# A paged-attention score loop: every second group of pages in partitions 32 to 127

## The chip, the core and the metric

The kernel runs on one core of a Trainium2 chip. TensorE (PE) multiplies into PSUM, VectorE (DVE) and ScalarE (ACT) move and compute, GpSimd (POOL) and SyncE (SP) issue transfers here. Sixteen DMA engines move the data between HBM and SBUF, whichever engine issues a transfer. The metric is the device time of one execution in microseconds (us), as the median of several runs. The profile comes from one further execution.

## The reference, cut to what matters

One inference step of a two-layer decoder: 512 prompt tokens and 8 sample tokens go through half feed-forward layers, a mixer and again a half feed-forward layer. The first layer's mixer has latent attention (MLA) beside a gated recurrence (HGRN2). For the 8 sample tokens the attention reads a paged cache of 4096 past positions each, 32 pages of 128 rows, found through a page table:

```python
q_lat = jnp.einsum('bshn,chn->bshc', q_nope, w_uk)
ckv_past = pool_ckv[layer_idx, page_table].reshape(db, -1, A_KV_LORA)     # 256 wide
kpe_past = pool_kpe[layer_idx, page_table].reshape(db, -1, A_ROPE)        # 32 wide
sc_past = (jnp.einsum('bshc,btc->bhst', q_lat, ckv_past)
           + jnp.einsum('bshr,btr->bhst', q_pe, kpe_past)).astype(jnp.float32) * SM_SCALE
...
p = jax.nn.softmax(jnp.concatenate([sc_past, sc_self], axis=-1), axis=-1).astype(ckv.dtype)
o_lat = (jnp.einsum('bhst,btc->bshc', p[..., :n_past], ckv_past)
         + jnp.einsum('bhst,btc->bshc', p[..., n_past:], ckv))
```

The score is a dot product over 256 + 32 = 288 rows. All data is float32.

## The kernel before

The time falls into three parts. Before about 550 us stand the first feed-forward layer, the input projection and the queries; after about 885 us the output projection, three feed-forward layers and the second mixer. Both are long rows of 128x128x260 matmuls on PE (L278 to L280), with weights that SP loads through three buffers (`stream`, L495). Between them, in some 330 us, the HGRN2 recurrence, the keys and values of the prompt and the prompt's attention run, and the whole cache is read beside them. The change touches only this middle part.

**Pages.** The host stores each page twice: transposed for the scores (three slices of 96 rows, `SR` = 96, `SK` = 3, so 96 partitions of 3 x 128 numbers) and as it is for the values (128 partitions of 256 numbers). A job is two pages (`JOB` = 2), a group is four jobs (`COLG` = 4), a sequence has four groups (`QUADS`), and there are 32 groups, here numbered 0 to 31. The score buffers `s_raw` and the value buffers `v_raw` are rings of eight jobs (`RING`), so of two groups: even groups lie in buffers 0 to 3, odd ones in 4 to 7.

**Who loads.** `load_job` (L457) issues one transfer per page, in `@block.sync` (SP) for all score pages and for every fourth job of value pages, in `@block.gpsimd` (POOL) for the other three. SP's order is fixed by the loop at `for k in range(COLG, S_JOBS + LAG)`: eight score transfers of a group n, then two value transfers of group n - 5 (`LAG` is 20 jobs), then group n + 1. Each score group starts with a wait on `s_done`, so with the scores of group n - 2, each pair of value transfers with a wait on `v_done`. Page numbers are read from SBUF into registers (`page_numbers`, L481).

**Who computes.** PE works through one list of instructions. `sample_to(k)` is called between the steps of the recurrence (`hgrn`), of the keys (`keys`) and of the prompt (`prompts`), and puts the scores of a group (L1685, 24 matmul records: three slices by four jobs, each job into its own 32 columns of the array), the values of a group (L1700) and steps of the softmax between them. During the recurrence that is one group in each of the 16 steps. The recurrence itself goes from PE (L1784) through eight dependent DVE operations (L1285) and back.

**Sample queries.** `sample_queries` on DVE clears `q_s` and fills it: the rotary rows (L1157), then three copies from PSUM (L1162). `q_s_ready` counts these to `Q_S_STEPS`; PE waits for it ahead of the first scores, POOL ahead of `state_in(0)`. These DVE operations stand just ahead of the recurrence's first DVE chain.

## Time and profile before

| | us |
|---|---|
| median of 3 runs (2272.53 to 2280.35) | 2275.16 |
| profiled execution, its own time | 2284.63 |
| its span, first to last instruction | 2282.9 |
| PE busy in the span | 2185.3 (96%) |
| DVE, ACT, POOL busy | 1036.6, 730.8, 120.2 |
| score pages loaded, 256 transfers of 144 KB | 37.7 MB |
| value pages loaded, 256 transfers of 128 KB | 33.6 MB |

The profiled execution is 9.5 us (0.4%) above the median and lies 1.7 us above its own span. In 40 slices of 57 us, PE is 90% busy or more except in slices 11 to 15 (571 to 856 us), the middle part, where the DMA engines' share goes up to its highest. An engine's busy time leaves out the issuing of transfers, so SP has no busy time at all in these views; what SP does is seen in the timeline and in the waits of the DMA queue's own engine.

### The profile page before, as it was taken

To read this page: it belongs to the slowest core of one execution; us is meant where nothing else is said; L and a number is where in the kernel's file an instruction comes from. 1 tells how busy PE (TensorE), PEld (TensorE's weight loads), DVE (VectorE), ACT (ScalarE), POOL (GpSimd) and SP (SyncE) were. 2 spreads that over 40 slices of the span, in tenths; PEclk is the share of its full clock that TensorE was granted. 3 is DMA by queue.
4 is the path that set the end of the run, shared out by engine and by line. 5 is a ranking of instruction groups with operands and counts; after the bars stand their busy time and mean duration, and the time that the engine had idled before them with its cause. 6 is when DMAs were issued, how large, how long until landed. Compare 5 with 4: busy or idle time off the path is not lost.

```text
span 2282.9 us, 46816 instructions
## 1 busy us (share of the span) xinstructions
PE 2185.3 (96%) x18285; PEld 2072.4 (91%) x18285; DVE 1036.6 (45%) x2002; ACT 730.8 (32%) x1292; POOL 120.2 (5%) x226
## 2 busy tenths in 40 slices
PE   8999999998776789999999999999999999999997
PEld 8999999997443458999999999999999999999997
DVE  5444434366654344544433444443446664444333
ACT  6222223354212333422222232222232233222222
POOL 0000000001234241000000000000000000000000
PEclk9999999998887789999999999999999999999999
DMA  4222223234799872222222222222322222222222
GB/s 162 92 92 92 92 102 100 81 125 147 213 265 279 236 212 93 84 92 92 92 92 100 97 91 91 92 92 92 102 92 92 92 93 92 88 87 91 94 100 75
DMA packets 101037, 261.98 MB, mean 115 GB/s; under 512 B 14385, under 2 KB 49218, under 8 KB 100866
## 3 DMA queue, kind: packets, MB, share of 16 engines
q1 hardware_dynamic: 89746, 228.83, 31.6%
q0 software_dynamic: 11184, 31.69, 4.7%
q8 instruction: 72, 1.18, 0.2%
q14 instruction: 35, 0.29, 0.0%
HBM read 255.29 MB, written 5.16 MB: 114 GB/s over the span
## 4 chain that ended last, share of the span: by engine, by line
PE 61%; DVE 1%; ACT 0%; issue 0%; DVEq 0%; ACTq 0%
PE bank L279 20%; PE bank L278 20%; PE bank L280 20%; PE bank L1929 1%; PE bank L1908 0%; PE bank L303 0%; DVE sb_x L1012 0%; PE bank L1921 0%; PE bank L1700 0%; PE bank L1943 0%; DVE sb_x L373 0%; ACT L312 0%; ACT sb_t L343 0%; DVE sb_h_lo L351 0%; ACT sb_h_hi L338 0%
## 5 line engine op out<-in xcount | busy, mean ns | idle before, releaser
L278 PE MATMUL bank<-sb_h_hi,sb_w_hi 128*128 128x260 f32 x3552 | 1005.9, 283 | 9.8 <-DVE sb_h_lo L1471 8.2
L279 PE MATMUL bank<-sb_h_lo,sb_w_hi 128*128 128x260 f32 x3552 | 1007.1, 284 | 0.0
L280 PE MATMUL bank<-sb_h_hi,sb_w_lo 128*128 128x260 f32 x3552 | 1003.8, 283 | 0.0
L250 ACT ACTIVATE sb_w_hi<-sb_raw 128x1024 fp32r<-128x1024 f32 x339 | 359.7, 1061 | 1260.8 <-PE bank L280 1257.1
L278 PEld LDWEIGHTS bank<-sb_h_hi,sb_w_hi 128*128 128x128 f32 x3552 | 668.5, 188 | 11.5 <-DVE sb_w_lo L256 8.3
L280 PEld LDWEIGHTS bank<-sb_h_hi,sb_w_lo 128*128 128x128 f32 x3552 | 671.4, 189 | 0.0
L279 PEld LDWEIGHTS bank<-sb_h_lo,sb_w_hi 128*128 128x128 f32 x3552 | 668.1, 188 | 0.2
L256 DVE TENSOR_TENSOR sb_w_lo<-sb_raw,sb_w_hi 128x1024 fp32r<-128x1024 f32 x339 | 415.3, 1225 | 382.4 <-ACT sb_w_hi L250 381.6
L279 PE MATMUL bank<-sb_a_lo,sb_w_hi 128*128 128x260 f32 x1408 | 399.1, 283 | 0.0
L278 PE MATMUL bank<-sb_a_hi,sb_w_hi 128*128 128x260 f32 x1408 | 398.7, 283 | 0.0
L280 PE MATMUL bank<-sb_a_hi,sb_w_lo 128*128 128x260 f32 x1408 | 397.7, 282 | 0.0
L280 PEld LDWEIGHTS bank<-sb_a_hi,sb_w_lo 128*128 128x128 f32 x1408 | 265.1, 188 | 0.0
L278 PEld LDWEIGHTS bank<-sb_a_hi,sb_w_hi 128*128 128x128 f32 x1408 | 264.9, 188 | 0.0
L279 PEld LDWEIGHTS bank<-sb_a_lo,sb_w_hi 128*128 128x128 f32 x1408 | 264.5, 188 | 0.0
L980 DVE TENSOR_TENSOR sb_t<-bank,sb_t 128x260 f32<-128x260 f32 x176 | 75.3, 429 | 261.1 <-PE bank L280 258.3
L972 DVE TENSOR_TENSOR sb_t<-bank,sb_r 128x260 f32<-128x260 f32 x176 | 74.4, 425 | 221.3 <-PE bank L280 200.7
L466 POOL DMA_DIRECT2D sb_v_raw<-in_cache x192 | 103.8, 541 | 195.0 <-PE bank L1700 176.2
L1685 PE MATMUL bank<-sb_s_raw,sb_q_s 96*32 96x256 f32 x768 | 60.1, 449 | 16.0 <-DMA sb_s_raw<-in_cache 8.8
L278 PE MATMUL bank<-sb_m_hi,sb_w_hi 128*128 128x260 f32 x256 | 73.2, 286 | 0.8 <-DVE sb_m_lo L1454 0.8
L279 PE MATMUL bank<-sb_m_lo,sb_w_hi 128*128 128x260 f32 x256 | 73.2, 286 | 0.0
L280 PE MATMUL bank<-sb_m_hi,sb_w_lo 128*128 128x260 f32 x256 | 73.0, 285 | 0.0
L985 DVE TENSOR_TENSOR sb_a_lo<-sb_t,sb_a_hi 128x260 f32 (+1 forms) x176 | 67.1, 423 | 0.0
(279 smaller groups left out, 1556.3 us busy)
## 6 DMA issues: line engine op xcount, KB each, us to landing
sb_raw<-in_w SPq DMA_DIRECT2D x339, 512.0 KB, 3.5
sb_s_raw<-in_cache SPq DMA_DIRECT2D x256, 144.0 KB, 4.7
sb_v_raw<-in_cache POOLq DMA_DIRECT2D x192, 128.0 KB, 5.3
sb_v_raw<-in_cache SPq DMA_DIRECT2D x64, 128.0 KB, 5.8
sb_x<-in_x SPq DMA_DIRECT2D x4, 520.0 KB, 6.2
out_y<-sb_x SPq DMA_DIRECT2D x8, 260.0 KB, 2.3
sb_st<-in_state POOLq DMA_DIRECT2D x8, 256.0 KB, 8.2
out_state_s<-sb_st POOLq DMA_DIRECT2D x8, 256.0 KB, 5.7
```

What stands on the lines that cost most here:

```text
L250: nc.scalar.activation(w_hi[slot][:], raw[slot][:], ACT.Copy).then_inc(S("w_hi_done"), 1)
L256: nc.vector.tensor_tensor(w_lo[slot][:], raw[slot][:], w_hi[slot][:], ALU.subtract).then_inc(S("w_lo_done"), 1)
L278: nc.tensor.matmul(out, wh, xh, start=first and c == 0, stop=False)
L279: nc.tensor.matmul(out, wh, xl, start=False, stop=False)
L280: mm = nc.tensor.matmul(out, wl, xh, start=False, stop=last and c == chunks - 1)
L466: eng.dma_start(slots[k % RING][0:rows, j, :], dram["cache"][bass.ds(page_numbers[j], 1), lo:lo + rows * width].rearrange("a (p w) -> (a p ...
L972: dve.tensor_tensor(t1[:, half[hf]], pair(g, hf), r[:, half[hf]], ALU.mult) \
L980: dve.tensor_tensor(t3[:, half[hf]], pair(g + 1, hf), t2[:, half[hf]], ALU.mult) \
L985: dve.tensor_tensor(a_lo[:, ff, half[hf]], t3[:, half[hf]], a_hi[:, ff, half[hf]], ALU.subtract) \
L1685: last = mm(out, q_s[0:SR, i, c, :], s_raw[(COLG * n + j) % RING][0:SR, :, c * P:(c + 1) * P], start=q % 2 == 0 and c == 0, stop=q % 2 == ...
L1929: last = mm(bank[3][:, b * P:(b + 1) * P], v_t[:, k, vals], prob_t[:, tri(b) + k, :], start=k == 0, stop=k == b)
```

## The change

Even groups stay as they are. A page of an odd group is loaded in two pieces: its rows 32 to 95 (64 rows) to partitions 32 to 95, and its rows 0 to 31 (32 rows) to partitions 96 to 127. Partitions 0 to 31 of buffers 4 to 7 are cleared once by POOL, and the scores of odd groups multiply over all 128 partitions. For this `q_s` gets a copy of its rows 0 to 31 in rows 96 to 127, by a fourth DVE copy. `Q_S_STEPS` goes up by one, and PE waits once for the clearing (`s_cleared`), ahead of group 1.

```diff
-        Q_S_STEPS = SK + 2
+        Q_S_STEPS = SK + 3
+        LOW = P - SR
...
             rows, lo, width = (SR, 0, S_W) if kind == "s" else (PAGE, SR * S_W, KV_LORA)
+            pieces = ((0, 0, rows),) if kind == "v" or k // COLG % 2 == 0 else ((LOW, LOW, SR - LOW), (SR, 0, LOW))
             for j in range(JOB):
-                eng.dma_start(slots[k % RING][0:rows, j, :],
-                              dram["cache"][bass.ds(page_numbers[j], 1), lo:lo + rows * width].rearrange("a (p w) -> (a p) w", w=width)) \
-                    .then_inc(loaded(kind, k), 16)
+                for to, row, count in pieces:
+                    first = lo + row * width
+                    eng.dma_start(slots[k % RING][to:to + count, j, :],
+                                  dram["cache"][bass.ds(page_numbers[j], 1), first:first + count * width].rearrange("a (p w) -> (a p) w", w=width)) \
+                        .then_inc(loaded(kind, k), 16)
...
-                eng.wait_ge(loaded("s", COLG * q), 16 * JOB * COLG * uses)
+                eng.wait_ge(loaded("s", COLG * q), 16 * JOB * COLG * uses * (1 + q % 2))
...
             state_in(1)
+            pool.wait_ge(S("half_done"), 2 * U0["ukv"])
+            for i in range(COLG, RING):
+                pool.memset(s_raw[i][0:LOW], 0.0).then_inc(S("s_cleared"), 1)
             pool.wait_ge(S("q_lat_mm"), 1)
...
+                dve.wait_ge(S("q_s_ready"), Q_S_STEPS - 1)
+                dve.tensor_copy(q_s[SR:P, :, :, 0:HEADS], q_s[0:LOW, :, :, 0:HEADS]).then_inc(S("q_s_ready"), 1)
...
+                rows = slice(0, SR if n % 2 == 0 else P)
+                if n == 1:
+                    pe.wait_ge(S("s_cleared"), COLG)
...
-                        last = mm(out, q_s[0:SR, i, c, :], s_raw[(COLG * n + j) % RING][0:SR, :, c * P:(c + 1) * P],
+                        last = mm(out, q_s[rows, i, c, :], s_raw[(COLG * n + j) % RING][rows, :, c * P:(c + 1) * P],
```

On SP, the start of group 1 (the first odd group) read as follows before. DMA rows name the buffer and the shape that is written; ISA rows are register work.

```order
L481 TENSOR_LOAD sb_pages_67 [waits half_done]
L466 ISA
L466 DMA sb_s_raw4_155<-in_cache 96x384
L466 ISA
L466 DMA sb_s_raw4_155<-in_cache 96x384
L466 ISA
L466 DMA sb_s_raw5_156<-in_cache 96x384
```

Now the same place reads:

```order
L485 TENSOR_LOAD sb_pages_67 [waits half_done]
L470 ISA
L470 DMA sb_s_raw4_155<-in_cache 64x384
L470 REGISTER_ALU
L470 DMA sb_s_raw4_155<-in_cache 32x384
L470 ISA
L470 DMA sb_s_raw4_155<-in_cache 64x384
L470 REGISTER_ALU
L470 DMA sb_s_raw4_155<-in_cache 32x384
L470 ISA
L470 DMA sb_s_raw5_156<-in_cache 64x384
```

Each page of an odd group is now two transfers, with a register operation ahead of each: 16 transfers a group where there were 8, and all 16 odd groups are like this one. The even groups are unchanged.

On DVE, the end of the sample queries and the start of the recurrence's chain (`sb_s_ring`) read before:

```order
L1157 COPY sb_q_s<-sb_q_t 32x8x8 [waits att_cleared]
L1162 COPY sb_q_s<-bank 96x8x8 [waits q_lat_mm]
L1162 COPY sb_q_s<-bank 96x8x8
L1162 COPY sb_q_s<-bank 64x8x8
L1282 COPY sb_s_ring<-bank 128x128 [waits state_mm]
L1285 SCALAR_TENSOR_TENSOR sb_s_ring<-sb_s_ring,sb_decay,bank 128x128 [waits state_step] x7
```

and now:

```order
L1169 COPY sb_q_s<-bank 96x8x8 [waits q_lat_mm]
L1169 COPY sb_q_s<-bank 96x8x8
L1169 COPY sb_q_s<-bank 64x8x8
L1172 COPY sb_q_s<-sb_q_s 32x24x8 [waits q_s_ready]
L1291 COPY sb_s_ring<-bank 128x128 [waits state_mm]
```

One copy with a wait for the copies before it stands between the sample queries and the recurrence. On POOL, between the loads of two sample states and the value pages of group 1, there are four new rows:

```order
L556 DMA sb_st1_120<-in_state 128x512
L580 MEMSET sb_s_raw4_155 32x768 [waits half_done]
L580 MEMSET sb_s_raw5_156 32x768
L580 MEMSET sb_s_raw6_157 32x768
L580 MEMSET sb_s_raw7_158 32x768
L485 TENSOR_LOAD sb_pages_67 [waits q_lat_mm]
```

The value pages of group 1 stand behind four clears on POOL; nothing else on POOL has moved.

## Rows read from the trace of the kernel before

**Rows 1.** Windows, whole core: length, busy us (count) per engine, PEclk, DMA share, GB/s

```profile
core 0: us, PE busy (x) PEld busy (x) DVE busy (x) ACT busy (x) POOL busy (x), PEclk, DMA share, GB/s
580.00:590.00 10.00, 7.73 (x94) 3.79 (x94) 5.71 (x17) 3.46 (x10) 0.00 (x0) 1.00 0.78 233
620.00:684.00 64.00, 49.62 (x544) 27.35 (x544) 33.06 (x105) 13.32 (x44) 24.17 (x45) 0.90 1.08 264
812.00:840.00 28.00, 22.81 (x224) 15.87 (x225) 11.47 (x37) 8.60 (x23) 12.12 (x22) 0.94 1.03 263
862.00:869.00 7.00, 5.75 (x54) 4.69 (x53) 4.01 (x15) 3.67 (x12) 3.20 (x6) 1.00 0.90 330
```

**Rows 2.** Waits of PE, 560 to 880 us: us in total, times, longest

```profile
PE bank L1784 <- DVE sb_s_ring L1285: 19.2, 10, 4.5
PE bank L1685 <- DMA sb_s_raw<-in_cache: 8.8, 5, 3.9
...
PE bank L1700 <- DMA sb_v_raw<-in_cache: 1.7, 2, 1.2
```

**Rows 3.** Timeline of SP, 616 to 690 us: start, length, transfers in a row

```profile
616.82 3.86 SPq L466 DMA_DIRECT2D sb_s_raw<-in_cache  x8
621.38 0.90 SPq L466 DMA_DIRECT2D sb_v_raw<-in_cache  x2
623.26 5.34 SPq L466 DMA_DIRECT2D sb_s_raw<-in_cache  x8
...
683.86 4.65 SPq L466 DMA_DIRECT2D sb_s_raw<-in_cache  x8
```

**Rows 4.** Waits of SP: 566 to 620, 620 to 684, 690 to 810, 809 to 830 us

```profile
SPq L466 <- PE bank L1685: 18.8, 6, 7.6
...
SPq L466 <- PE bank L1685: 12.8, 8, 2.8
...
SPq L466 <- PE bank L1685: 47.6, 10, 9.6
...
SPq L466 <- PE bank L1685: 5.4, 1, 5.4
```

**Rows 5.** Transfers of score pages, 620 to 684 us: issue ns, and time to landing

```profile
L466 SPq DMA_DIRECT2D sb_s_raw<-in_cache x59: 317/317/1424, 619.9 to 683.9; - x59
...
DMA to landing us min/median/max: 5.0/8.0/11.2
```

**Rows 6.** Timeline of DVE, POOL and PE, 556 to 603 us

```profile
556.55 0.52 DVE L1162 COPY sb_q_s<-bank 96x64 f32<-96x64 f32 x3
...
559.53 3.52 POOL L466 DMA_DIRECT2D sb_v_raw<-in_cache  x6 [0.82 <-issue]
602.48 1.13 POOL L466 DMA_DIRECT2D sb_v_raw<-in_cache  x2 [39.43 <-PE bank L1700]
...
560.05 2.08 PE L1784 MATMUL bank<-sb_v_blk,sb_kdv 64*128 64x512 f32 x4 [4.50 <-DVE sb_s_ring L1285]
570.25 1.48 PE L1685 MATMUL bank<-sb_s_raw,sb_q_s 96*32 96x256 f32 x24
```

**Rows 7.** POOL's memset of 128x1024; score and value matmuls, ns min/median/max

```profile
L581 POOL MEMSET sb_q_bd<- x1: 971/971/971, 690.2 to 690.2; 128x1024 f32 x1
...
L1685 PE MATMUL bank<-sb_s_raw,sb_q_s x768: 376/379/636, 563.7 to 840.4; 96*32 96x256 f32 x192
...
L1700 PE MATMUL bank<-sb_v_raw,sb_p_t x512: 376/379/634, 600.6 to 871.2; 128*32 128x256 f32 x171
```

**Rows 8.** Timeline of SP and PE, 809 to 832 us: groups 29, 30 and 31

```profile
809.40 3.95 SPq L466 DMA_DIRECT2D sb_s_raw<-in_cache  x8
814.04 0.90 SPq L466 DMA_DIRECT2D sb_v_raw<-in_cache  x2
815.68 4.28 SPq L466 DMA_DIRECT2D sb_s_raw<-in_cache  x8
820.66 1.03 SPq L466 DMA_DIRECT2D sb_v_raw<-in_cache  x2
822.43 5.12 SPq L466 DMA_DIRECT2D sb_s_raw<-in_cache  x8
828.24 0.90 SPq L466 DMA_DIRECT2D sb_v_raw<-in_cache  x2
...
829.91 1.56 PE L1685 MATMUL bank<-sb_s_raw,sb_q_s 96*32 96x256 f32 x24 [3.91 <-DMA sb_s_raw<-in_cache]
```

## The prediction

> **What bounds the kernel now.** Outside 550 to 885 us PE is 90% busy or more, and the change touches nothing there. Inside, I read the windows first: the DMA engines are saturated from 620 to 684 us (share 1.08, 264 GB/s) and again from 812 to 840 us (1.03, 263 GB/s) [rows 1]. The page transfers are what fills them: a group is 8 x 144 KB of scores and 8 x 128 KB of values, 2.23 MB, and at 264 GB/s that takes 8.4 us. Then the waits of PE: in 320 us it stands 8.8 us for score pages and 1.7 us for value pages, together 10.5 us, and 19.2 us for the recurrence on DVE [rows 2]. So the DMA engines are full for a stretch, but PE idles little for them directly. All that a perfect transfer could give back is about those 10.5 us, 0.5% of the kernel.
>
> The third view is SP, which no busy time shows. From 616.82 to 683.86 us it starts eight groups, one in 67.0 / 8 = 8.4 us [rows 3]. In each it spends 3.86 us on eight score transfers (0.50 us from one issue to the next, of which the transfer instruction is 0.317 us [rows 5] and the rest register work), 0.90 us on two value transfers, and 0.7 us on page numbers ahead of each. Some blocks are longer (5.34 instead of 3.86 us), since a single issue can take up to 1.42 us. Its free time is what it waits for the scores of two groups back: 12.8 us between 620 and 684 us [rows 4]. So SP works (67.0 - 12.8) / 8 = 6.8 us of each 8.4 us. It is the second engine here with hardly any room.
>
> **What the change does to SP.** This is the term that decides. Odd groups get 8 more issues. A 96-row transfer costs 0.50 us from issue to issue. Smaller pieces are not in the trace; fewer rows might take a little less, long issues come in proportion. The bounds are 0.42 us (the instruction's 0.317 us and half of the register work) and 0.55 us (0.50 us and a share of long issues); I take 0.48 us, nearer to the row that there is, with 0.25 us of long issues in a group: 8 x 0.48 + 0.25 = 4.1 us more per odd group, 2.05 us per group. Four stretches:
> - 566 to 616.82 us, groups 2 to 8 on SP: three odd ones add 12.3 us. SP's waits there are 18.8 - 7.6 = 11.2 us (the longest, 7.6 us, lies before group 2) [rows 4]. It starts the saturated stretch 12.3 - 11.2 = 1.1 us late at least, and not all free time is where it is needed: I take 1.5 us (1 to 4).
> - 616.82 to 684 us: 6.8 + 2.05 = 8.85 us of work per group against the 8.4 us between groups: 0.5 us x 8 groups = 4 us (at 0.42 us an issue 6.8 + 1.7 = 8.5, so 1 us; at 0.55 us with the long issues 6.8 + 2.4 = 9.2, so 6.5 us). PE's next scores wait for these pages, the pages two groups on wait for the scores, and so the delay stays.
> - 690 to 810 us: SP waits 47.6 us [rows 4]; six odd groups at most add 25 us. Covered by the keys' and prompt's work on PE: 0 (0 to 1).
> - 809 to 829 us: SP's only wait (5.4 us) lies ahead of group 29 [rows 4, 8]. Then it works through to 829.14 us, and odd groups 29 and 31 add 4.1 us each. The pages of group 30 would be issued by 824.1 instead of 820.0 us; PE took them at 829.91 us, after a wait of 3.91 us [rows 8]. 5.8 us is more than the smallest time to landing but less than the median of 8.0 us [rows 5]. I take 1.3 us (0 to 3).
>
> **The other parts.** The copy of `q_s` on DVE stands ahead of the chain for which PE waits 4.50 us at 560.05 us [rows 6], so it counts in full. Three copies of 64 numbers take 0.52 us [rows 6]; one of 192 with a wait for its predecessors is 0.2 to 0.6 us: 0.4 us. The four clears on POOL: 768 numbers each, against 971 ns for 1024 [rows 7], so 0.73 x 4 = 2.9 us. They delay the value pages of group 1 from 559.53 us, behind which POOL idles 39.43 us [rows 6]: nothing. They end by 563 us, and PE's scores of group 1, which now wait for them, start at 570.25 us [rows 6]: nothing. Matmuls over 128 instead of 96 partitions: 379 ns in both rows [rows 7], nothing. What an extra transfer costs the DMA engines themselves has no row: 16 transfers share a group's 8.4 us, 0.53 us each, and since the bytes stay the same, the 8 extra ones lie between 0 and half of that, 2.1 us per odd group or 1.05 per group. I take 0; the upper end, 8.4 + 1.05 = 9.5 us, belongs to the third rival.
>
> **What the balance of partitions may give.** Between 580 and 590 us only score pages move: 233 GB/s at share 0.78, so 299 GB/s for full engines. Between 862 and 869 us only value pages, over 128 partitions, move: 330 / 0.90 = 367 GB/s [rows 1]. So 96-partition transfers run slower than 128-partition ones by 19% per byte. But SP then needs 8.85 us for it, so the gain stays out of reach. In the sum: 0 (-1 to 0).
>
> A rule that speaks for the change is in "DMA: Bandwidth & Descriptors" (Issuing engines are not separate DMA queues): the sequencer's time to initiate a transfer is usually small beside the transfer. Here eight issues take 3.86 us and their 1.18 MB at 299 GB/s take 3.95 us: the trace does not agree. By that rule SP's terms would vanish and the sum would be about 0.4 us.
>
> **The sum.** 1.5 + 4 + 0 + 1.3 + 0.4 = 7.2 us. The profiled execution's 2284.6 us would become 2291.8 us. It stands 9.5 us above the median of its runs, and I put the same difference on the median: 2275.2 + 7.2 = 2282.4 us, 0.32% slower. About 0.3% (6.8 us) is what a measurement of this kernel can tell from no change, so the forecast sits on that edge.
>
> **The rivals.**
> - *Slack covers the issues.* SP waits some 77 us between 566 and 830 us [rows 4], and 15 groups x 4.1 us is 62 us. If issues of small pieces are cheap (0.42 us), or DMA backlog (8.0 us to landing [rows 5]) hides them, the first two stretches lose 1 us each: 2277 us (2275 to 2280). Against it: the free time is where it isn't needed.
> - *The transfers balance, and the time falls.* Place: the saturated stretches. Eight and three groups, 0.8 us each, are 9 us, and not above the 10.5 us of [rows 2]: 2267 us (2264 to 2270). It decides from an issue cost at which SP's work per group is below 7.6 us, that is 8 extra issues in 1.6 us, 0.2 us each. The instruction alone is 0.317 us, so this needs smaller pieces to be issued much faster, or DMA backpressure to be a large part of SP's 6.8 us.
> - *Dearer pieces.* 0.55 us an issue and twice as many long issues, or 1.05 us more per group on the DMA engines: either makes 9.5 us a group, 1.1 us x 8 = 9 us, with 3 us ahead of it and 3 us behind: 2290 us (2286 to 2295).
> - *It doesn't do what it says*: odd groups stay lopsided the other way. This changes the sum by under 1 us.
>
> **How the numbers follow.** Forecast 0.46 (2279 to 2286: half above the edge and half below, a bit more above, 0.27 to 0.19), slack 0.26, faster 0.10, dearer 0.18. Slower by over 0.3%: 0.27 + 0.18 = 0.45. Within 0.3%: 0.19 + 0.26 = 0.45, of the gain case 0.02 more: 0.47. Faster: 0.08. The range leaves out most of the gain case and the upper end of the dear one: 2270 to 2291 us.
>
> **What the profile after would show.** SP's row for an odd group: 16 transfers in 7.7 us, not 3.86 us. SP's waits between 620 and 690 us: down from 12.8 us to nearly nothing, and PE's wait for score pages up from 8.8 us. Eight groups from 616 us on in 71 us instead of 67 us. PE's scores still 379 ns. The DMA share between 620 and 684 us below 1.0 would show that SP and no longer the engines sets the pace; GB/s well above 264 would show that balancing works and prove me wrong. I am also wrong if an odd group's issues take 5 us, or if transfers of 32 rows land later than those of 96.

## The result, and the profile after

The changed kernel takes 2320.35 us (median of 4 runs, 2316.18 to 2321.31), the kernel before on the same chip 2275.52 us (2272.53 to 2280.35): ratio 1.0191, 95% interval 1.0170 to 1.0213. That is 45 us by the medians and 43 us by the ratio, 2% slower, six times the 7.2 us of the forecast and outside its range. The side was right, the size was not. Each kernel below was measured beside the kernel before again, on its own chip (medians of before 2276.42 to 2278.26 us), so compare the ratios rather than the times.

The profiled execution's span grew from 2282.9 to 2318.8 us, by 35.9 us (the profiled run of before lay above its median, this one doesn't, so the spans differ by less than the medians). All of it arises in the middle part, 560 to 956 us of the new trace. The windows of both kernels over the same work, before and then after (columns as in [rows 1]):

```profile
560.00:920.00 360.00, 292.28 (x2631) 186.05 (x2632) 170.89 (x498) 105.99 (x272) 109.49 (x203) 0.85 0.78 213
```

```profile
560.00:956.00 396.00, 301.29 (x2630) 186.47 (x2631) 171.29 (x499) 106.38 (x272) 110.97 (x206) 0.82 0.65 195
```

PE does the same work (2631 and 2630 matmuls in the records) in 36 us more: it idles 27.0 us longer (94.7 instead of 67.7 us) and is busy 9.0 us longer, at a mean granted clock of 0.82 instead of 0.85. The busy part is in the score matmuls: they are busy for 71.7 us instead of 60.1. Their median is 631 ns and not 379 as in [rows 7]. Even and odd groups are alike in it (means of 517 and 521 ns), so it isn't the 128 partitions. 418 of the 768 records take some 631 ns, where 201 did before, which goes with the lower granted clock:

```profile
L1697 PE MATMUL bank<-sb_s_raw,sb_q_s x768: 376/631/637, 563.9 to 876.1; 96*32 96x256 f32 x96, 128*32 128x256 f32 x96
```

What PE idles for stands in its waits, 560 to 930 us, the answer to [rows 2]:

```profile
PE bank L1697 <- DMA sb_s_raw<-in_cache: 36.1, 12, 6.1
PE bank L1796 <- DVE sb_s_ring L1294: 18.6, 9, 5.3
...
PE bank L1712 <- DMA sb_v_raw<-in_cache: 3.0, 4, 1.0
```

Score pages: 36.1 us instead of 8.8, which is 27.3 us and so about the whole of the longer idle time. The waits for the recurrence and for the value pages changed by 0.6 us less and 1.3 us more. Why the pages are late is seen on SP (its timeline, the answer to [rows 3]; L470 is the old L466):

```profile
622.77 3.86 SPq L470 DMA_DIRECT2D sb_s_raw<-in_cache  x8
627.33 0.90 SPq L470 DMA_DIRECT2D sb_v_raw<-in_cache  x2
628.97 11.23 SPq L470 DMA_DIRECT2D sb_s_raw<-in_cache  x16
640.90 0.90 SPq L470 DMA_DIRECT2D sb_v_raw<-in_cache  x2
642.54 4.26 SPq L470 DMA_DIRECT2D sb_s_raw<-in_cache  x8
...
649.14 11.49 SPq L470 DMA_DIRECT2D sb_s_raw<-in_cache  x16
...
662.98 3.86 SPq L470 DMA_DIRECT2D sb_s_raw<-in_cache  x8
```

An even group still takes 3.86 us, or a little more. The odd ones shown take 11.2 to 11.5 us, where the prediction had 7.7; all sixteen lie between 10.7 and 13.0 us, with a median of 11.2. From 622.77 to 662.98 us SP starts two pairs of groups, 20.1 us for each (20.4 over the four pairs from group 9 to group 17), against 16.8 us before. SP's waits (560 to 890 us) show that this is its limit; it hardly waits for anything any more, while before it waited 79.1 us for scores in 560 to 840 us:

```profile
SPq L470 <- PE bank L1697: 6.6, 5, 2.5
SPq L470 <- PE bank L1712: 5.2, 2, 4.0
```

And the DMA engines, saturated before at 1.08 and 264 GB/s [rows 1], are not any more; a score page that is issued lands after 2.6 us instead of 8.0 [rows 5]. The windows and the landing times of score pages between 620 and 684 us:

```profile
620.00:684.00 64.00, 44.03 (x434) 22.42 (x438) 29.57 (x89) 11.95 (x39) 19.31 (x36) 0.83 0.73 216
...
DMA to landing us min/median/max: 1.8/2.6/4.3
```

So the bound of this stretch moved from the DMA engines to the engine that starts their transfers. The last group's scores on PE start at 873.99 us; they started at 839.31 us. The profile's loss is nearly complete there, 34.7 of 35.9 us.

### The profile page after: what moved, and what is told of

Its sections match the earlier page's. It is cut to its first block, busy times and chain, and to the rows that moved or that the text cites. A ratio compares the mean times of both kernels' runs of the same rounds, so it can differ in the third digit from the quotient of the medians.

```text
span 2318.8 us, 47206 instructions
## 1 busy us (share of the span) xinstructions
PE 2194.0 (95%) x18285; PEld 2073.1 (89%) x18285; DVE 1036.6 (45%) x2003; ACT 730.6 (32%) x1292; POOL 122.4 (5%) x230
## 3 DMA queue, kind: packets, MB, share of 16 engines
q8 instruction: 72, 1.18, 0.2%
## 4 chain that ended last, share of the span: by engine, by line
PE 60%; DVE 1%; ACT 0%; issue 0%; DVEq 0%; ACTq 0%
PE bank L279 20%; PE bank L278 20%; PE bank L280 19%; PE bank L1941 1%; PE bank L1920 0%; PE bank L303 0%; DVE sb_x L1019 0%; PE bank L1933 0%; PE bank L1712 0%; PE bank L1955 0%; DVE sb_x L373 0%; ACT L312 0%; ACT sb_t L343 0%; DVE sb_h_lo L351 0%; ACT sb_h_hi L338 0%
## 5 line engine op out<-in xcount | busy, mean ns | idle before, releaser
L470 POOL DMA_DIRECT2D sb_v_raw<-in_cache x192 | 103.4, 539 | 231.6 <-PE bank L1712 212.8
L1697 PE MATMUL bank<-sb_s_raw,sb_q_s 96*32 96x256 f32 (+1 forms) x768 | 71.7, 519 | 43.1 <-DMA sb_s_raw<-in_cache 36.1
L1697 PEld LDWEIGHTS bank<-sb_s_raw,sb_q_s 96*32 96x32 f32 (+1 forms) x768 | 30.4, 142 | 72.8 <-issue 30.5
```

The source lines that it names most:

```text
L470: eng.dma_start(slots[k % RING][to:to + count, j, :], dram["cache"][bass.ds(page_numbers[j], 1), first:first + count * width].rearrange("a ...
L1697: last = mm(out, q_s[rows, i, c, :], s_raw[(COLG * n + j) % RING][rows, :, c * P:(c + 1) * P], start=q % 2 == 0 and c == 0, stop=q % 2 == ...
```

## The experiments

The first question was which part of the change costs so much. **Theory:** SP's time for the smaller pieces. **Rivals:** the destination from partition 32 on, the clearing, copying and 128-row matmuls, or the larger number of transfers as such. Three kernels do one part each, and a fourth tries several cuts.

**split_in_place: two pieces, but where the rows lay before.**

```diff
+            pieces = ((0, rows),) if kind == "v" or k // COLG % 2 == 0 else ((0, 64), (64, 32))
```

> The kernel before, with one thing of the change: the pages of odd groups come in two pieces (64 and 32 rows), but each row stays in the partition it had (0 to 95), with no copy of the queries, no clears, matmuls over 96 partitions. Theory A (the time is SP's issuing of twice the transfers for odd groups): nearly the whole loss, 2312 to 2322 us; an odd group's 16 issues take 11 us as in the changed kernel, and PE's waits for score pages are again above 30 us. Theory B (the destination in partitions 32 to 127, or the rows' new places, make the pieces dear): the pieces issue in 0.5 us each, 7.7 us per odd group, and the time is 2278 to 2286 us. Theory C (matmuls, copy and clears cost it): 2275 us.

Measured: 2310.64 us (2309.13 to 2311.99), ratio 1.0142 (1.0124 to 1.0161). The cutting alone costs 32 us, just under the range of theory A. An odd group's 16 transfers on SP take 10.1 to 12.3 us, and typically:

```profile
627.48 10.41 SPq L469 DMA_DIRECT2D sb_s_raw<-in_cache  x16
```

PE waits 36.5 us for score pages, as in the change.

**one_piece: other partitions, but one transfer.** The host stores rows 0 to 31 of each score page once more behind row 95, so that rows 32 to 127 of the stored page go to partitions 32 to 127 in one transfer of 96 rows. All the rest is as in the change.

```diff
-            rows, lo, width = (SR, 0, S_W) if kind == "s" else (PAGE, SR * S_W, KV_LORA)
-            pieces = ((0, 0, rows),) if kind == "v" or k // COLG % 2 == 0 else ((LOW, LOW, SR - LOW), (SR, 0, LOW))
+            rows, lo, width = (SR, 0, S_W) if kind == "s" else (PAGE, P * S_W, KV_LORA)
+            pieces = ((0, 0, rows),) if kind == "v" or k // COLG % 2 == 0 else ((LOW, LOW, SR),)
```

> The change with one transfer instead of two: the host stores a score page's rows 0 to 31 a second time behind row 95, so rows 32 to 127 of that are loaded at once into partitions 32 to 127 of the odd groups' buffers. Copy, clears and matmuls over 128 partitions as in the change. Theory A: an odd group's eight issues take 3.9 us again and the time is 2270 to 2277 us, lower than before only by what the balance of partitions gives. Theory B: the issue costs about 0.6 us or more instead of 0.5 us, an odd group's eight issues 5 us or more, and the time is 2277 to 2285 us. If balancing works, the 620 to 684 us stretch moves over 280 GB/s instead of 264; if each odd group is as lopsided as before, 264 GB/s and no change.

Measured: 2278.75 us (2274.14 to 2282.80), ratio 1.0003 (0.9990 to 1.0015). Its window, to be held against the first window of [rows 1] over the same stretch:

```profile
620.00:684.00 64.00, 49.10 (x532) 26.61 (x532) 32.99 (x105) 13.20 (x44) 24.02 (x45) 0.88 1.08 266
```

266 GB/s at the same share 1.08: in the other partitions the pages move as fast as they did, so alternation gives nothing, and it costs nothing either. The eight issues of an odd group take 3.92 us, as theory A had it. The median lies 1.75 us above A's range and inside B's, but B's dear issue is not there, and the ratio can't be told from 1.

**rest_only: all but the transfers.** Odd groups are loaded as before, into partitions 0 to 95; partitions 96 to 127 of buffers 4 to 7 are cleared, `q_s` is copied, and odd groups' matmuls take 128 partitions, the upper 32 of them against zeros.

```diff
-            pieces = ((0, 0, rows),) if kind == "v" or k // COLG % 2 == 0 else ((LOW, LOW, SR - LOW), (SR, 0, LOW))
+            pieces = ((0, 0, rows),)
...
-                pool.memset(s_raw[i][0:LOW], 0.0).then_inc(S("s_cleared"), 1)
+                pool.memset(s_raw[i][SR:P], 0.0).then_inc(S("s_cleared"), 1)
```

> The change without its transfers: odd groups' pages are loaded in one transfer to partitions 0 to 95 as before, partitions 96 to 127 are cleared, the queries are copied and odd groups multiply over 128 partitions. Theory A: 2275 to 2277 us, the 0.4 us of the copy is all there is. Theory C: several us of loss, with longer matmul records in odd groups.

Measured: 2278.28 us (2272.66 to 2283.82), ratio 1.0007 (0.9994 to 1.0020). These parts are not to be seen in the time; the 1.3 us above the range of theory A are within the interval. Its window shows how much such a figure can differ by chance, since here every transfer is as it was before:

```profile
620.00:684.00 64.00, 49.75 (x520) 26.36 (x523) 32.59 (x102) 13.07 (x43) 23.38 (x44) 0.86 1.08 258
```

258 GB/s against 264 [rows 1] with the same transfers: a difference of some 2% between two such windows means nothing by itself.

**forms: odd groups cut in other ways.** On the storage of one_piece, a different cut from odd group to odd group, each with a source line of its own.

```diff
+                if form == 2:
+                    eng.dma_start(*piece(j, 32, 64)).then_inc(loaded(kind, k), 16)
+                    eng.dma_start(*piece(j, 96, 32)).then_inc(loaded(kind, k), 16)
...
+                if form == 4:
+                    eng.dma_start(*piece(j, 32, 48)).then_inc(loaded(kind, k), 16)
+                    eng.dma_start(*piece(j, 80, 48)).then_inc(loaded(kind, k), 16)
```

> A look at the price of an issue by its form. The layout with the doubled rows, and odd groups that load partitions 32 to 127 in different forms: 96 rows at once, 64+32, 32+64, 48+48, 80+16, 16+80. All rows arrive. If the count of rows sets the price, equal counts cost the same wherever they start (64 rows about 0.53 us and 32 rows 0.44 us of instruction time, 96 rows 0.32 us); if the start partition does, 96 rows from partition 32 cost 0.53 us; if only the second piece's register work does, all are 0.32 us.

Measured: 2298.84 us in one run. The instructions of one line: ns min/median/max of one issue. L477 is 96 rows from partition 32 on, L479 and L480 are 64 and 32 rows (the change's own pieces), L482 and L483 32 and 64 rows, L485 and L486 48 and 48 rows, L492 80 rows and L491 16 rows:

```profile
L477 SPq DMA_DIRECT2D sb_s_raw<-in_cache x24: 317/318/460, 552.5 to 846.6; - x24
...
L479 SPq DMA_DIRECT2D sb_s_raw<-in_cache x24: 524/525/657, 571.8 to 796.1; - x24
...
L480 SPq DMA_DIRECT2D sb_s_raw<-in_cache x24: 324/430/1047, 572.7 to 796.8; - x24
...
L482 SPq DMA_DIRECT2D sb_s_raw<-in_cache x24: 315/430/442, 588.4 to 815.1; - x24
...
L483 SPq DMA_DIRECT2D sb_s_raw<-in_cache x24: 474/477/1360, 588.9 to 815.8; - x24
...
L485 SPq DMA_DIRECT2D sb_s_raw<-in_cache x24: 315/316/332, 608.3 to 833.3; - x24
...
L486 SPq DMA_DIRECT2D sb_s_raw<-in_cache x24: 315/316/817, 608.8 to 833.8; - x24
```

Neither a short piece nor a start at partition 32 is dear by itself. The cuts with 64 rows in them are, by 110 to 210 ns for each of the two instructions, and 64 rows cost 525 ns from partition 32 on and 477 from 64 on, so neither the row count nor the start alone sets the price. That gave the next pair to compare: the same number of transfers, cut 48 and 48.

**split48: split_in_place with 48 and 48 rows.**

```diff
-            pieces = ((0, rows),) if kind == "v" or k // COLG % 2 == 0 else ((0, 64), (64, 32))
+            pieces = ((0, rows),) if kind == "v" or k // COLG % 2 == 0 else ((0, 48), (48, 48))
```

> The kernel before, with each score page of the odd groups loaded in two pieces of 48 rows (partitions 0 to 47 and 48 to 95, where they lay before) instead of the 64 and 32 rows of split_in_place; nothing else is changed, nothing is copied or cleared. As many transfers as in the change and in split_in_place. Theory A, the price hangs on the number of rows of a transfer: 48 rows were issued in 315 ns in the kernel with several forms, so the 16 issues of an odd group take 8.1 us (10.4 to 10.8 us in split_in_place), 4.1 us more than a whole group's 3.86 us. That is the very sum of the prediction, and the kernel should come out near it: 2277 + 5 to 15 us, ratio 1.002 to 1.007; score-page waits of PE 12 to 20 us between 560 and 930 us. Rival B, what costs is that there are 16 transfers instead of 8 (their completion, the small packets of the semaphores, the queue's ring): the kernel stays at the 2310 us of split_in_place, ratio 1.014.

Measured: 2286.68 us (2283.79 to 2294.84), ratio 1.0046 (1.0027 to 1.0065), where 64 and 32 rows had 1.0142. SP's timeline and the window:

```profile
630.79 4.28 SPq L469 DMA_DIRECT2D sb_s_raw<-in_cache  x8
635.76 0.90 SPq L469 DMA_DIRECT2D sb_v_raw<-in_cache  x2
637.41 8.93 SPq L469 DMA_DIRECT2D sb_s_raw<-in_cache  x16
...
648.67 3.86 SPq L469 DMA_DIRECT2D sb_s_raw<-in_cache  x8
```

```profile
620.00:684.00 64.00, 47.26 (x491) 25.84 (x490) 31.91 (x100) 12.52 (x41) 23.60 (x44) 0.85 0.91 250
```

PE waits 14.5 us for score pages. Time and waits are as theory A had them; the blocks of 16 issues take 7.8 to 9.6 us, since some issues are long. Two thirds of the loss by cutting hang on where the cut is, and a third (about 10 us) on there being twice as many transfers. This is also the kernel that the prediction's arithmetic is about: 16 issues at 0.50 us, some 8.8 us of SP per group, about 7 us in all. Whether its loss is SP's time is asked again below (split48_vpool).

**before_busy: SP's time alone.** No transfer is changed. The page number of every score page from group 1 on is read into the register right ahead of its own transfer.

```diff
+                number = page_numbers[j] if page_numbers is not None else numbers_of(eng, k, 1)[0][j]
...
-                    if k % 4 == 0:
-                        numbers = page_numbers(sp, k, 4)
-                    load_job(sp, "s", k, numbers[k % 4])
+                    load_job(sp, "s", k, None)
```

> The kernel before, with the page number of each score page from group 1 on read into SP's register anew right ahead of its transfer (one read per page, eight per group) instead of one read for the eight pages of a group. The transfers, their number, shape and order stay as they were. A read took 470 to 531 ns in the trace of before, about 0.53 us with what lies around it, so SP gets 7 x 0.53 = 3.7 us more work per group, 7.4 us per pair of groups: what the change's dearer issues add (some 7.4 us per odd group). Theory A, the change's loss is SP's time and nothing else: this kernel is as slow as the change, 2305 to 2322 us, ratio 1.013 to 1.020, PE waits for score pages 25 to 60 us between 560 and 930 us, and the DMA share between 620 and 684 us falls to 0.7 to 0.8. Rival B, the loss hangs on the 16 transfers (their completion, their packets, their pieces landing later): a mere delay on SP costs little, under 10 us, as long as each transfer is one of 96 rows.

Measured: 2310.50 us (2308.83 to 2310.82), ratio 1.0143 (1.0120 to 1.0166). Waits of PE and the window:

```profile
PE bank L1686 <- DMA sb_s_raw<-in_cache: 26.5, 10, 5.4
```

```profile
620.00:684.00 64.00, 45.44 (x430) 23.32 (x433) 28.71 (x87) 11.56 (x37) 19.78 (x37) 0.82 0.79 229
```

The transfers are as large and as many as before, and some 32 us are lost, with the same picture as in the change: share 0.79, clock 0.82. Delay on SP is enough for these 32 us; dear or numerous transfers are not needed for them. The other 11 us of the change are not shown by this run. Part of them is that the delay came out smaller: a group's eight issues take 7.34 us instead of 3.86, so 7.0 us more per pair and not 7.4.

**after_vpool and before_vpool: SP relieved.** POOL issues all value pages; SP issues none and reads none of their numbers.

```diff
-                if k >= LAG and (k - LAG) % 4 == 3:
-                    if k - LAG == RING - 1:
-                        sp.wait_ge(S("q_lat_mm"), 1)
-                    load_job(sp, "v", k - LAG, page_numbers(sp, k - LAG, 1)[0])
...
-                    numbers = page_numbers(pool, COLG * quads[0], 3)
-                    for j in range(3):
+                    numbers = page_numbers(pool, COLG * quads[0], 4)
+                    for j in range(4):
```

> The change, with all value pages issued by GpSimd (POOL); SP issues none of them (before: two of a group's eight value pages, with their page numbers, some 1.6 us of SP per group). Theory A, the change loses its 45 us because SP issues 16 dear transfers per odd group: SP's work per pair of groups falls from 20 to 16.8 us, about the 17 us that a pair took in the kernel before, so most of the loss comes back: 2280 to 2295 us, ratio 1.002 to 1.009. Rival B, the loss is in the DMA engines or in when the pages land: relief of SP changes little, 2312 us or more. Rival C: POOL has no room for two more issues per group, and the value pages become late instead; PE's wait for value pages, 3.0 us in the changed kernel, would rise above 10 us.

> Control for the run of the change with all value pages issued by POOL: the kernel before with that one edit. Theory A, SP isn't what bounds the kernel before (PE waits 8.8 us for score pages, the DMA engines are saturated): ratio 1.000 within 0.003, 2270 to 2283 us. Rival B, SP already bounds the saturated stretch (6.8 us of work in 8.4 us, unevenly): 3 to 8 us faster, ratio 0.997 to 0.9985. Rival C, POOL becomes the bound: slower by 5 us or more with PE waiting for value pages.

Measured: the kernel before with this edit 2280.11 us, ratio 1.0006 (0.9990 to 1.0021); the change with it 2298.37 us, 1.0088 (1.0063 to 1.0112). The edit alone gives nothing, since SP is not yet the bound there. In the change it gives back 22 of 45 us by the medians, 23 of 43 by the ratios. PE's wait for score pages falls from 36.1 to 27.0 us, value pages are not among its larger waits, so POOL has the room. The time is 3 us above the range of theory A, which expected more to come back. SP's timeline, 620 to 664 us:

```profile
619.67 44.34 SPq L470 DMA_DIRECT2D sb_s_raw<-in_cache  x59
```

59 issues in 44.34 us are 18.0 us for the 24 of a pair, not 16.8. SP waits only 2.5 us between 620 and 684 us, and the DMA share is 0.90, so SP still sets the pace.

**split48_vpool: cheap cut and SP relieved.** The edits of split48 and before_vpool together.

> split48 (score pages of odd groups in two pieces of 48 rows, in place) with all value pages issued by POOL as in before_vpool. SP's work per group: 6.8 + 2.05 = 8.9 us in split48, less the 1.6 us for value pages = 7.3 us, under the 8.4 us that the saturated DMA engines need. Theory A, split48's 10 us are SP's time: they vanish, 2275 to 2282 us, ratio 0.999 to 1.002, and the DMA share between 620 and 684 us is 1.0 or more again (0.91 in split48). Rival B, part of the 10 us is what 8 more transfers cost the DMA engines: 2284 to 2288 us remains, with the share at 1.0 or more and GB/s under 260.

Measured: 2287.15 us (2282.90 to 2292.25), ratio 1.0045 (1.0033 to 1.0058). Theory A failed here and rival B's forecast came in: the 10 us of split48 did not vanish, though SP has time again (it waits 9.6 us between 620 and 684 us, none in split48). The windows of before_vpool and of this kernel:

```profile
620.00:684.00 64.00, 49.40 (x532) 27.27 (x534) 32.62 (x104) 13.19 (x44) 31.88 (x60) 0.86 1.01 265
```

```profile
620.00:684.00 64.00, 48.40 (x510) 26.75 (x508) 32.75 (x104) 13.18 (x44) 32.23 (x61) 0.86 1.00 255
```

Against before_vpool, which differs in the cut alone, 7 to 9 us are lost (1.0045 against 1.0006, two intervals that don't touch). SP's time hardly accounts for them, as it has waits to spare; what is left is the eight more transfers in an odd group while the DMA engines are full, a term that the prediction put at nothing. How they cost it is not shown. The engines move 4% less at about the same share, which over the 11 groups of the saturated stretches would be 4 us (0.34 us each), but rest_only shows 2% less with unchanged transfers, so much of the 4% may be chance.

This changes the reading of split48. There SP hardly waits, and a pair of groups takes 17.9 us; with SP relieved a pair takes 17.7 us, and the time stays. What fits both runs is two limits of about the same height, SP's time and the cost of the transfers themselves, so that taking the first away shows the second. No run separates the two further.

**all_high: every group in partitions 32 to 127.** one_piece for even groups too, with all eight buffers cleared.

```diff
-            pieces = ((0, 0, rows),) if kind == "v" or k // COLG % 2 == 0 else ((LOW, LOW, SR),)
+            pieces = ((0, 0, rows),) if kind == "v" else ((LOW, LOW, SR),)
```

> The host stores rows 0 to 31 of each score page once more behind row 95, and every group, odd or even, is loaded in one transfer of 96 rows to partitions 32 to 127; all eight buffers are cleared below, all score matmuls take 128 partitions. (one_piece does this for odd groups alone.) Theory A, which partitions 96 rows go to makes no difference and nothing is gained from alternating: 2275 to 2281 us, ratio 1.000 within 0.002, DMA share 620 to 684 us 1.08 with 264 GB/s within 4. Rival B, alternating does balance something in one_piece (2278.75 us) which the copy or the clears eat up: with all groups on one side the saturated stretches get longer, by 0.4 to 0.8 us a group or 5 to 9 us in all, 2284 to 2288 us.

Measured: 2276.44 us (2268.11 to 2281.11), ratio 0.9986 (0.9968 to 1.0004). The window has 271 GB/s at share 1.08, above the 264 within 4 of theory A. rest_only was 6 below before with unchanged transfers, so such a difference doesn't speak for the partitions. All groups on one side, all on the other, or taking turns (one_piece): the same time within what can be told. There was no balance to be had by turns of whole groups.

**forms2 and forms3: what exactly is dear.** The kernel before, odd groups cut in place, the cut changing from odd group to odd group; forms3 also cuts 64 rows by columns into two halves of 768 bytes a row.

```diff
+                if pieces == ((0, 32), (32, 32), (64, 32)):
+                    eng.dma_start(*one(*(0, 32))).then_inc(loaded(kind, k), 16)
+                    eng.dma_start(*one(*(32, 32))).then_inc(loaded(kind, k), 16)
+                    eng.dma_start(*one(*(64, 32))).then_inc(loaded(kind, k), 16)
```

> The kernel before, with the odd groups' score pages cut in place into pieces of other sizes, a different cut from odd group to odd group: 72+24 rows, 88+8, 56+40, 32+32+32, 64+16+16, 32+64. It is for the duration of one issue instruction on SP by number of rows; its whole time says little. Theory A, the dear ones are pieces of exactly 32 or 64 rows, wherever they stand and whatever follows: 24, 40, 56, 72, 88, 8 and 16 rows take 316 ns, 32 rows 430 to 440 ns in each of the three places, 64 rows 475 ns in partition 0 and on and about 525 ns from partition 32 on. Rival B, counts that don't divide evenly over 16 engines are dear too: 24, 40, 56, 72, 88 and 8 rows above 400 ns. Rival C, it is the alternation of two sizes that costs: three pieces of 32 rows in a row take 316 ns, and 72+24 is dear.

> The kernel before, with the odd groups' score pages cut in place, again for the duration of one issue instruction on SP and not for the whole time: 60+36 rows, 68+28, 64 rows in two halves of 192 columns and then 32 rows, 63+33, 65+31, 64+8+24. Theory A, a transfer of exactly 64 rows of 1536 bytes is dear (475 ns from partition 0) and makes the next one dear too, whatever its size (442 ns instead of 316), and its neighbours in size are not: 60, 63, 65 and 68 rows about 320 ns or less, 36, 28, 33 and 31 rows about 280 to 316 ns; in 64+8+24 the 64 rows 475 ns, the 8 rows 400 ns or more (277 ns behind 88 rows), the 24 rows 302 ns. Rival B, it is a band of sizes from 57 to 71 rows: 60, 63, 65 and 68 rows above 400 ns. The halves of 64 rows have no forecast from A or B: 475 ns would say that the row count alone decides, 316 ns that the bytes take part (48 KB each, as 32 full rows).

forms2, in this order: the second of three pieces of 32 rows (L487); then 64 rows (L490), 16 rows (L491) and 16 rows (L492), issued in a row:

```profile
L487 SPq DMA_DIRECT2D sb_s_raw<-in_cache x24: 315/316/1303, 602.5 to 859.6; - x24
...
L490 SPq DMA_DIRECT2D sb_s_raw<-in_cache x16: 474/475/596, 623.3 to 763.3; - x16
...
L491 SPq DMA_DIRECT2D sb_s_raw<-in_cache x16: 401/442/782, 624.0 to 763.9; - x16
...
L492 SPq DMA_DIRECT2D sb_s_raw<-in_cache x16: 315/316/746, 624.6 to 764.5; - x16
```

Theory A was right on 64 rows and wrong on 32. Pieces of 32 rows among themselves take 316 ns. The 442 ns stand for whatever follows a transfer of 64 rows: 16 rows right behind it take 442 ns, the next 16 rows 316 ns. The other counts of forms2 took 277 ns (8 rows), 303 (24), 287 (40), 320 (56), 305 (72) and 297 (88), so rivals B and C are refuted.

forms3, in this order: 63 rows (L485); the left and the right half of 64 rows (L481, L482); 65 rows (L488):

```profile
L485 SPq DMA_DIRECT2D sb_s_raw<-in_cache x24: 277/278/694, 613.7 to 894.2; - x24
...
L481 SPq DMA_DIRECT2D sb_s_raw<-in_cache x24: 468/480/1179, 589.2 to 875.8; - x24
L482 SPq DMA_DIRECT2D sb_s_raw<-in_cache x24: 468/468/930, 590.0 to 876.5; - x24
...
L488 SPq DMA_DIRECT2D sb_s_raw<-in_cache x16: 313/1762/3532, 631.2 to 786.1; - x16
```

60 rows took 328 ns and 68 rows 255. It is 64 exactly and no band of sizes, and it is the number of rows and not the bytes, since the halves are as dear. One part of theory A failed: 8 rows behind 64 took 338 ns and not 400 or more, so the surcharge of the follower is smaller for a smaller one. The 65 rows start at 313 ns and then stall for 1.7 to 3.5 us, a different matter (see the last section). The whole times (2310.03 and 2347.51 us, one run each) mix all cuts.

## Why the prediction was wrong

**What bounds the kernel: right.** That SP is "the second engine here with hardly any room" is what decided. SP's waits went to almost nothing, the DMA share fell below 1, and PE's wait for score pages rose, as the prediction's last part had it. Two signs there failed: PE's scores did not stay at 379 ns, as said above, and eight groups took 81.4 us (628.97 to 710.40) and not 71.

**The term that failed: the price of a small piece's issue.** The step reads "A 96-row transfer costs 0.50 us from issue to issue ... fewer rows might take a little less", with bounds 0.42 and 0.55 us. Measured are 0.71 us for the 64-row piece and 0.65 us for the 32-row piece behind it (medians): 1.37 us for a page that cost 0.50. The 16 issues of an odd group take 11.2 us instead of 7.7, some 7.4 us more than an even group's 3.86 and not 4.1. The upper bound was set by one shape's duration with a margin for long issues. It had no room for a shape whose instruction itself takes longer. The rival "dearer pieces" stopped at the same 0.55 us.

Where the price is 0.50 us, in split48, the loss is 10 us (1.0046) beside the 7.2 us forecast. That does not prove the rest of the working: with SP relieved the loss stays, so a second term, the extra transfers' own cost, stands behind SP's. That the sum came close there is partly luck.

**How the error grew.** The four stretches by SP's timeline, where the later start of a group is what the stretch ahead of it cost. In before, group 9 starts at 616.82 us, group 17 at 683.86 [rows 3], group 29 at 809.40 [rows 8]. After:

```profile
628.97 11.23 SPq L470 DMA_DIRECT2D sb_s_raw<-in_cache  x16
...
710.40 10.84 SPq L470 DMA_DIRECT2D sb_s_raw<-in_cache  x16
...
837.88 11.18 SPq L470 DMA_DIRECT2D sb_s_raw<-in_cache  x16
```

| stretch of before | forecast | measured | the prediction's sum with 7.4 for 4.1 us |
|---|---|---|---|
| to 616.82 us | +1.5 | +12.2 | 3 x 7.4 - 11.2 = +11.0 |
| to 683.86 us | +4 | +14.4 | 4 x 7.4 - 12.8 = +16.8 |
| to 809.40 us | 0 | +1.9 | 6 x 7.4 - 47.6, below 0 |
| to the scores of group 31 on PE | +1.3 | +6.2 | 2 x 7.4 = 14.8, see below |
| sum | +6.8 | +34.7 | |

So one wrong number explains the first three stretches to within 3 us, in the form that the prediction gave them: extra issue time less the slack. 3.3 us more per odd group meant little as long as there was slack, and counted in full when it was gone: the first stretch went from 1.1 to 11.0 us. The slack between 690 and 810 us did absorb, as forecast: SP's waits there fell from 47.6 us [rows 4] to 2.9, by 44.7 us, and six odd groups bring 6 x 7.4 = 44.4. In the last stretch SP's own last issue ends 13.6 us later, but in before PE came to these scores only 11.8 us after it and now 4.3, since the pages land after 2.4 us instead of 9.1; that leaves 6.2 us.

The ruler is no finer than some us. The trace of before belongs to one of its longest executions (2284.63 us, where the medians are near 2277). Against the trace of rest_only, which loads every page as before did, the four stretches cost 12.9, 11.8, 8.4 and 8.7 us, 41.8 in all, nearer to the 43 us of the ratio. How much the third stretch absorbed is therefore known only roughly, 36 to 42 of the 44 us.

The kernels side by side, with the time from one pair of groups to the next on SP, waits included (mean of the four pairs from group 9 to group 17), and the loss by the ratio:

| kernel | us from pair to pair | lost, us |
|---|---|---|
| before | 16.8 | 0 |
| rest_only | 17.4 | 2 |
| split48_vpool | 17.7 | 10 |
| split48 | 17.9 | 10 |
| after_vpool | 17.9 | 20 |
| split_in_place | 19.7 | 32 |
| before_busy | 19.9 | 33 |
| after | 20.4 | 43 |

The order is the same in both columns, with ties, but the first column can't price the second: kernels that lose nothing clear of noise lie between 16.3 us (all_high) and 17.4 us, and of two kernels at 17.9 one loses twice as much. after_vpool is already 8.7 us behind before_vpool when it starts group 9, ahead of these pairs.

**PE's clock: argued, not shown.** PE is busy 9.0 us longer, at a granted clock of 0.82 instead of 0.85, after it had idled more; before_busy has 0.82 too between 620 and 684 us (0.90 before [rows 1]), with nothing changed but SP's delay. But SP sets the pace, and PE waits for its pages, so slower matmuls should mostly fill time in which PE would wait. They could still count where SP waits for PE, and that is 11.8 us between 560 and 890 us. No run held the clock to test it.

**Parts that were right.** Clears (757 ns each; 0.73 us was said), `q_s` copy (0.25 us; 0.4 said) and 128-partition matmuls: together 1.0007 in rest_only. Balance at nothing: 1.0003 in one_piece. In the working of the balance, the window from 862 to 869 us was read as value pages alone; three transfers of 512 KB of weights are issued within it or just ahead of it, so the 19% per byte is not a clean comparison. Nothing in the sum hung on it. **Also wrong:** the extra transfers' own cost on the DMA engines, taken at 0. With 48 and 48 rows and SP relieved it is some 7 to 9 us; whether it adds to SP's delay in the change, where the DMA share is only 0.73, is not shown.

The difference between split_in_place and the change is 11 us by the ratios and 8.7 us between the two profiles. A page's two issues take 1.37 us in the change and 1.29 us in place, as the 64-row instruction takes 530 ns into partition 32 and on and 475 ns into partition 0 and on, and the register work is 30 ns more. That is 0.69 us per odd group, just the difference between 19.7 and 20.4 us per pair, and over the nine odd groups of the stretches without slack 6 us. The rest is open.

**The rivals.** "Dearer pieces" named the right mechanism at too small a price (0.55 us an issue and 2290 us). "Slack covers the issues" is refuted by the time, "the transfers balance" by one_piece and all_high.

## What to carry to other kernels

When an engine that only starts transfers has little time to spare, as SP here with 1.6 of 8.4 us, read the duration of the issue instruction for the very shape that the change introduces. If the trace has none, let the upper bound be a multiple and not a margin: a page's two issues cost 1.37 us here where 0.96 us was expected. Work out as well what a dearer price costs once the slack is gone: here 4.1 us per odd group were to cost 7 us in all, and 7.4 us cost 43. And a delay of that kind can be tried without the change, by giving the issuing engine more work of its own; before_busy gave 32 of the 43 us. And when relieving the engine gives nothing back, as in split48_vpool, look for a second limit of the same height before you call the first one innocent.

## What the runs showed of the hardware

**A transfer of exactly 64 rows is dear to issue on SP, and so is the one behind it.** 475 to 477 ns into partitions 0 to 63 or 64 to 127, 525 to 530 ns into 32 to 95, 468 to 480 ns at half the row width; the next transfer takes 430 to 443 ns with 16 or 32 rows and 338 ns with 8. No run says why.

**For the other row counts the price follows the largest divisor up to 16.** Median ns of one issue on SP, from forms, forms2 and forms3:

| largest divisor up to 16 | rows of the transfer | ns |
|---|---|---|
| 1 | 31 | 238 |
| 4 | 68 | 255 |
| 8, 9 | 8; 63 | 277; 278 |
| 10, 11 | 40; 33, 88 | 287; 295, 297 |
| 12 | 24, 36, 72 | 303, 303, 305 |
| 14, 15 | 28, 56; 60 | 320; 328 |
| 16 | 16, 32, 48, 80, 96 | 316 to 318 |

64 rows have the divisor 16 as well and cost half as much again.

**Row counts that divide badly can stall the issuing engine.** In the group cut 65 and 31, the first four issues of 65 rows take 0.31 to 0.37 us and the next ones 1.7 to 3.5 us; 63 and 33 rows don't show it (at most 1.2 us). It looks like a queue that has filled up, which no view shows directly. The Trainium skill, "DMA: Bandwidth & Descriptors" (Why a DMA increments its semaphore by 16 and not by 1), says that a transfer is spread over the largest number of engines up to 16 that divides its rows: 31 rows would then all go through one engine, 65 through thirteen, 63 through nine and 33 through eleven. The traces agree in their packets under 512 bytes. The change has 128 transfers more than the kernel before, all with row counts that 16 divides, and 2049 more such packets, so 16 for each. If each transfer has one such packet per engine that it uses, the rule gives 1992 more for forms2 and 1464 for forms3. The pages of the profile have 16377 and 15849 against 14385, which is 1992 and 1464.

**Issue time against data time.** An odd group's 16 issues take 11.23 us for the same 1.18 MB that take 3.95 us at 299 GB/s. The Trainium skill, "DMA: Bandwidth & Descriptors" (Issuing engines are not separate DMA queues), says that the time to initiate a transfer is usually small beside the transfer. For one transfer by itself this trace agrees, 0.7 us beside the 2.6 us to landing. For a row of them from one engine it doesn't: there issue time counts against data time, and the issues take almost three times as long.
